# A streaming encoder step on one core: a table of step places for each engine instead of one shared plan

## What is computed

```
for each of 2 layers:
  u = rmsnorm(x) @ w_in                     # one projection, split over three head groups
  oa = softmax(q1 k1) v - lam softmax(q2 k2) v        # group A, 6 heads, block-causal mask
  score = sum_h w_h relu(qi_h . ki);  sel = top_k(score, 256)
  ob = softmax(q k[sel]) v[sel]                       # group B, 5 heads, keys picked by an indexer
  S, oc = gated linear recurrence in blocks           # group C, 5 heads
  x += concat(rmsnorm(oa), ob, rmsnorm(oc) silu(g)) @ w_out
  a, gate = rmsnorm(x) @ w_up;  x += (silu(conv3(a)) * gate) @ w_down
y = rmsnorm(x)
```

## Time and profile before

| | |
|---|---|
| median of 3 runs | 3888.84 us (3884.03 to 3899.14) |
| the profiled execution | 3897.18 us, span 3895.3 us |
| TensorE busy | 3691.7 us, 95% |
| VectorE, ScalarE, GpSimd busy | 2065.7, 1263.7, 761.1 us |
| mean granted clock of TensorE | 0.971 |
| DMA | 339.55 MB |

### The profile page before, as it was taken

How to read it: one execution, slowest core, us unless ns; L and a number is a source line. 1 busy time by engine, 2 the same in 40 slices (tenths; PEclk the granted TensorE clock), 3 DMA queues, 4 the chain that set the end, 5 groups by cost and what they waited for, 6 DMA issues and landing times. The chain is left out here.

```text
span 3895.3 us, 54785 instructions
## 1 busy us (share of the span) xinstructions
PE 3691.7 (95%) x21676; PEld 2940.2 (75%) x21676; DVE 2065.7 (53%) x4711; ACT 1263.7 (32%) x2918; POOL 761.1 (20%) x812
## 2 busy tenths in 40 slices
PE   7997799999999999999999999999999999999998
PEld 5775577678777777778867777787777787788887
DVE  1674564376635554428846555067644654553442
ACT  1124333245243432222244333145344433312221
POOL 2200211111010133202000013323001011453334
PEclk9998898999999999999999999999999999999999
DMA  4332222322121223233231222335112122342223
GB/s 146 97 109 65 77 87 78 103 95 92 56 84 36 78 89 96 80 113 124 72 101 48 82 68 88 107 114 162 55 48 87 30 84 65 96 141 87 67 84 94
DMA packets 151608, 339.55 MB, mean 87 GB/s; under 512 B 30312, under 2 KB 68648, under 8 KB 138040
## 3 DMA queue, kind: packets, MB, share of 16 engines
q1 hardware_dynamic: 151352, 336.04, 27.7%
HBM read 299.31 MB, written 36.68 MB: 86 GB/s over the span
## 5 line engine op out<-in xcount | busy, mean ns | idle before, releaser
L1042 PE MATMUL PS<-xn,wring 128*128 128x272 f32 (+1 forms) x7168 | 1693.7, 396 | 24.9 <-DVE xn L1598 15.1
L1042 PEld LDWEIGHTS PS<-xn,wring 128*128 128x128 f32 x7168 | 1381.1, 195 | 288.6 <-issue 35.3
L2010 POOL TENSOR_TENSOR xT<-xT,res 128x272 f32<-128x272 f32 (+1 forms) x320 | 255.6, 800 | 2251.3 <-ACT res L1325 2211.4
L1042 PE MATMUL PS<-dense,wring 128*128 128x256 f32 (+1 forms) x2816 | 654.6, 390 | 10.4 <-ACT res L1325 5.1
L1042 PEld LDWEIGHTS PS<-dense,wring 128*128 128x128 f32 x2816 | 532.1, 192 | 106.7 <-issue 10.3
L1325 ACT ACTIVATE res<-PS 128x272 f32<-128x272 f32 (+1 forms) x320 | 123.6, 388 | 539.5 <-PE PS L1042 514.0
L1063 PE MATMUL PS<-wring,xn 128*128 128x256 f32 (+1 forms) x1152 | 266.3, 392 | 2.3 <-ACT dense L1339 2.3
L1063 PEld LDWEIGHTS PS<-wring,xn 128*128 128x128 f32 (+1 forms) x1152 | 214.4, 188 | 49.5 <-issue 5.9
L1042 PE MATMUL PS<-catT,wring 128*128 128x272 f32 (+1 forms) x1024 | 235.5, 391 | 4.7 <-issue 2.7
L1333 ACT ACTIVATE dense<-PS 128x256 f32<-128x256 f32 (+1 forms) x176 | 68.3, 389 | 521.7 <-PE PS L1042 480.9
L1042 PEld LDWEIGHTS PS<-catT,wring 128*128 128x128 f32 x1024 | 195.2, 192 | 44.8 <-issue 11.3
(11 more groups left out here) (243 smaller groups left out, 4492.7 us busy)
## 6 DMA issues: line engine op xcount, KB each, us to landing
wring<-in_wu SPq DMA_DIRECT2D x88, 1024.0 KB, 4.9
wring<-in_wf SPq DMA_DIRECT2D x88, 512.0 KB, 3.7
wring<-in_wo SPq DMA_DIRECT2D x64, 512.0 KB, 3.6
wring<-in_wd SPq DMA_DIRECT2D x96, 320.0 KB, 2.9
wring<-in_wd SPq DMA_DIRECT2D x64, 384.0 KB, 3.1
wring<-in_wn SPq DMA_DIRECT2D x16, 1024.0 KB, 5.5
kv<-out_projT SPq DMA_DIRECT2D x48, 256.0 KB, 4.2
out_projT<-dense SPq DMA_DIRECT2D x40, 272.0 KB
```

The source lines that it names most:

```text
L1042: mm = nc.tensor.matmul(PS[:, dbank(t.g0), 0:cw], wtile(t.q, i), rhs, start=(kk == a), stop=(kk == b - 1))
L2010: nc.gpsimd.tensor_tensor(x, x, res[:, i % NRES, 0:cw], ALU.add).then_inc(s_res, 1)
```

## The change

`PLAN` becomes a dictionary of three strings, one for each engine, and `both` takes the engine's name. TensorE's string comes from `TURNS_BEFORE`, which gives for each of the 540 steps the number of dense turns ahead of it. ScalarE's and VectorE's add the entries of `SCALAR_LATER` and `VECTOR_LATER` to it (a negative entry puts the step ahead). The old string remains as `LOADS` and feeds `STEPS_AT` alone, so SyncE's order is what it was; GpSimd's program isn't touched, and no instruction is added or removed.

```diff
-PLAN = "".join((
+LOADS = "".join((
...
-for _x in PLAN:
+for _x in LOADS:
...
+TURNS_BEFORE = {
+    ("X", 0): (
+        30, 31, 31, 31, 31, 31, 32, 32, 35, 35, 35, 35, 35, 35, 35, 38, 38, 41, 41, 41, 42, 49, 51, 51, 52, 52, 52, 52, 52, 52, 53, 54, 54, 54, 54,
+        54, 54, 54, 55, 55, 65, 65, 65, 66, 66, 66, 66, 66, 66,
+    ),
+    ("B", 0): (
+        66, 66, 66, 66, 66, 66, 66, 66, 66, 66, 66, 66, 67, 67, 67, 67, 67, 67, 67, 68, 68, 68, 68, 68, 68, 70, 70, 71, 71, 76, 76, 77, 77, 77, 78,
+        79, 81, 81, 81, 81, 82, 83, 83, 83, 84, 86, 87, 89, 90, 90, 90, 90, 91, 91, 92, 93, 94, 94, 94,
+    ),
...
+SCALAR_LATER = {
...
+    ("C", 0): (
+        -1, 1, 1, 0, -1, 0, -3, 0, -3, -1, -3, 0, 3, -1, 0, -1, -1, -1, -2, -2, -4, -1, 0, -1, 0, -1, -1, -1, -2, -1,
+    ),
...
+def order_of(later):
+    plan, done = "", 0
+    for step in STEPS:
+        for n, d in zip(TURNS_BEFORE[step], later[step] if later else (0,) * len(TURNS_BEFORE[step])):
+            plan, done = plan + "d" * (n + d - done) + "s", n + d
+    return plan + "d" * (len(TURNS) - done)
+
+PLAN = {"pe": order_of(None), "act": order_of(SCALAR_LATER), "dve": order_of(VECTOR_LATER)}
...
-        def both(turns, steps):
-            for x in PLAN:
+        def both(turns, steps, which):
+            for x in PLAN[which]:
...
-                both(dense_tensor(pe), (None for kind, m in STEPS for _ in make[kind](pe, m)))
+                both(dense_tensor(pe), (None for kind, m in STEPS for _ in make[kind](pe, m)), "pe")
```

More of the change, by code:

```diff
@@ new lines @@
+SCALAR_LATER = {
+    ("X", 0): (
+        -4, -1, -1, 7, 7, 8, 9, 9, 6, 6, 6, 6, 6, 6, 6, 3, 3, 1, 1, 1, 1, -6, -6, -6, -6, -6, -6, -6, -1, -1, -1, -1, -1, 0, 3, 3, 3, 3, 2, 4, -6,
+        -6, -5, -6, -4, -2, -2, -2, -2,
+    ),
+    ("B", 0): (
+        -2, -2, -2, -2, -2, -2, -2, -2, -2, -2, 0, 0, -1, -1, -1, -1, -1, -1, -1, -2, -2, -1, 0, 0, 0, -1, 1, 2, 2, -1, -1, 0, 0, 0, -1, -1, -1, -1,
+        -1, -1, -1, 0, 0, 0, 1, -1, 0, -1, -1, 0, 0, 0, 0, 0, 0, 0, 0, 0, 0,
+    ),
+    ("C", 0): (
+        -1, 1, 1, 0, -1, 0, -3, 0, -3, -1, -3, 0, 3, -1, 0, -1, -1, -1, -2, -2, -4, -1, 0, -1, 0, -1, -1, -1, -2, -1,
+    ),
+    ("M", 0): (
+        -1, -1, -2, -4,
+    ),
+    ("X", 1): (
+        -2, -1, 0, 0, 0, 0, 0, 0, 0, 0, 0, -1, 2, 1, -2, 6, 5, 7, 7, 12, 13, 13, 14, 16, 13, 14, 13, 15, 15, 16, 14, 9, 10, 6, 10, 8, 8, 8, 11, 11,
+        13, 11, 13, 17, 21, 15,
+    ),
+    ("B", 1): (
+        11, 8, 6, 0, -1, -1, 0, -1, -1, -1, 0, 0, 0, -1, -1, 0, 1, 0, 4, 0, 0, 0, -1, 0, 0, 0, 0, 0, 0, -1, 1, 0, 1, 0, 1, 0, 1, -1, -1, -1, 1, -1,
+        2, 0, 1, 0, 0, 2,
+    ),
+    ("C", 1): (
+        0, 6, 5, 1, -2, -2, -2, 1, -1, -1, -5, -1, -3, -1, -1, -1, -1, 0, -1, -1, 0, 2, -1, 1, -8, -5, -1, -1, -1, -1,
+    ),
+    ("M", 1): (
+        -1, -1, -2, -2,
+    ),
+    ("X", 2): (
+        -1, -1, -1, -6, -5, -5, -5, -4, -4, -3, 1, 2, 4, 5, 5, 7, 6, 6, 5, 5, 5, 4, 1, -4, -4, -4, -1, 0, 2, 2, 4, 4, 5, 5, 6, 6, 3, 3, 3, 3, 3, 3,
+        6, 13, 12, 11, 7, 4, 4,
+    ),
+    ("B", 2): (
+        4, 3, 1, -1, -1, -1, 1, 0, 0, 0, -2, -2, -2, -2, -2, 0, 0, 0, 0, 0, 0, 0, 0, 0, 0, -1, 0, -1, -1, 0, -1, 0, -1, 1, 1, 0, 0, 0, -1, -2, -1,
+        -1, -1, -1, -1, -1, -2, -2, -1, 0, 0, -1, 0, 0, -1, 1, -1, 0, -1,
+    ),
+    ("C", 2): (
+        2, 1, 1, 0, 0, 0, 0, 0, -2, -3, 0, -1, 0, 0, -1, -1, -1, 5, -1, -1, -1, 3, 3, 0, 1, -1, -3, -3, -3, -4,
+    ),
+    ("M", 2): (
+        -4, 4, 1, 3,
+    ),
+    ("X", 3): (
+        0, 0, -1, -1, 0, 2, 0, -1, -1, -2, -4, -5, -11, -9, -9, -12, -11, -11, -12, -17, -16, -16, -14, -13, -13, -13, -12, -12, -16, -18, -19, -23,
+        -21, -24, -22, -21, -23, -20, -22, -20, -15, -14, -13, -12, -11, -7,
+    ),
+    ("B", 3): (
+        -1, 0, 1, 0, -1, -1, 0, 0, 1, -1, 0, -1, -1, 0, -1, -1, 0, 0, 0, 0, -1, -1, -1, 0, 0, 0, -1, 0, 1, 0, 0, -1, -1, -1, 0, -1, -1, 0, -1, 0, 0,
+        0, 2, 0, 0, 0, 0, 1,
+    ),
+    ("C", 3): (
+        0, 1, 4, 0, -1, -1, 0, -1, -1, -2, -2, 0, -2, 0, -4, -2, -2, -1, -2, 1, 0, -1, -1, -1, -1, -8, -5, -4, -3, -1,
+    ),
+    ("M", 3): (
+        -3, -1, 0, 8,
+    ),
+}
@@ new lines @@
+VECTOR_LATER = {
+    ("X", 0): (
+        -7, -6, -6, -6, -1, 10, 9, 9, 8, 8, 8, 8, 8, 9, 11, 11, 11, 13, 17, 17, 17, 10, 8, 8, 8, 10, 13, 14, 14, 14, 13, 12, 13, 13, 13, 13, 13, 16,
+        15, 15, 5, 5, 5, 4, 4, 4, 4, 4, 4,
+    ),
+    ("B", 0): (
+        4, 4, 4, 4, 5, 5, 5, 5, 5, 5, 5, 5, 4, 4, 4, 4, 4, 4, 4, 3, 3, 3, 3, 3, 3, 1, 1, 0, 1, -3, -3, -3, -3, -3, -4, -2, 1, 1, 2, 2, 7, 6, 10, 10,
+        9, 7, 6, 8, 7, 7, 7, 11, 10, 10, 9, 8, 7, 7, 7,
+    ),
+    ("C", 0): (
+        7, 9, 9, 10, 10, 11, 9, 9, 6, 6, 1, 1, 1, -3, -6, -7, -7, -7, -9, -7, -9, -9, -9, -9, -10, -12, -11, -8, -9, -8,
+    ),
+    ("M", 0): (
+        -8, -8, -10, -9,
+    ),
+    ("X", 1): (
+        -10, -2, -2, -4, -4, -1, 0, 1, 3, 3, 3, -4, -1, 2, 0, 4, 7, 8, 8, 9, 12, 12, 13, 17, 14, 15, 13, 14, 15, 16, 14, 8, 8, 4, 11, 16, 15, 15, 15,
+        15, 15, 15, 15, 15, 19, 11,
+    ),
+    ("B", 1): (
+        7, 4, 4, -2, -3, -3, -1, -2, 0, -1, -2, -1, -1, -1, 5, 5, 11, 9, 8, 4, 2, 1, 2, 1, 0, 3, 1, 0, -2, -2, -2, 10, 13, 11, 7, 2, 2, 1, 0, 1, 0,
+        1, 2, 7, 4, 2, 2, 1,
+    ),
+    ("C", 1): (
+        2, 6, 5, 5, 5, 8, 9, 18, 25, 34, 37, 36, 33, 34, 31, 30, 29, 28, 27, 26, 26, 25, 22, 20, 14, 18, 18, 18, 17, 17,
+    ),
+    ("M", 1): (
+        16, 15, 14, 11,
+    ),
+    ("X", 2): (
+        9, 9, 9, 1, 1, -1, -3, -3, -3, -4, -4, -6, -6, -6, -6, -5, -3, -3, -2, 0, 1, 2, -1, -2, 0, 0, -1, -1, -1, -3, -2, -2, -1, 0, 0, 0, -2, 2, 3,
+        4, 4, 4, 4, 5, 4, 4, 0, -1, 3,
+    ),
+    ("B", 2): (
+        4, 4, 2, 4, 4, 3, 3, 4, 4, 4, 1, 1, 2, 3, 3, 3, 3, 3, 3, 3, 2, 2, 2, 2, 2, 1, 0, 1, 1, 1, 1, 0, -1, 1, -2, 2, 0, -2, 1, 0, 1, 1, 1, 1, 0, 0,
+        0, 0, 0, 0, 0, 1, 0, -1, 1, 0, 6, 6, 5,
+    ),
+    ("C", 2): (
+        5, 3, 3, 0, 0, -2, -2, -2, -4, -3, -1, 6, 4, 2, -3, 0, 1, 1, -4, -3, 2, 3, 5, -4, -4, -4, -4, 0, -4, -7,
+    ),
+    ("M", 2): (
+        -3, 3, 15, 17,
+    ),
+    ("X", 3): (
+        6, 10, 9, 20, 17, 16, 12, 11, 9, 8, 6, 3, -5, -5, -5, -8, -8, -9, -12, -17, -10, -8, -8, -8, -5, -5, -5, -4, -3, -3, -5, -10, -10, -13, -13,
+        -13, -16, -16, -18, -18, -13, -13, -10, -6, -4, -3,
+    ),
+    ("B", 3): (
+        -1, -1, -1, -2, -4, -1, 0, 0, 1, 0, -1, -1, -2, -1, -2, -1, -1, 0, 0, 0, -1, -2, 0, 2, 0, 8, 7, 5, 1, 1, 0, -3, -2, -1, 0, -1, -1, -2, 1, 2,
+        0, -2, 3, 4, 1, -1, -4, -1,
+    ),
+    ("C", 3): (
+        -1, 5, 5, 1, -1, -1, 0, 2, 0, 1, 2, 3, 3, 6, 1, 1, 1, 3, 2, 5, 4, 2, 2, 1, -2, 0, 0, 0, 3, 1,
+    ),
+    ("M", 3): (
+        -1, 2, 2, -5,
+    ),
+}
@@ L2076, in _ @@
                 nc.scalar.activation(lam2, lam2, ACT.Exp).then_inc(s_pre_exp, 1)
-                both(dense_scalar(act), (None for kind, m in STEPS for _ in make[kind](act, m)))
+                both(dense_scalar(act), (None for kind, m in STEPS for _ in make[kind](act, m)), "act")
             @block.vector
@@ L2109, in _ @@
                 dve.wait_ge(s_set, 1)
-                both(dense_vector(dve, step), (None for kind, m in STEPS for _ in make[kind](dve, step, m)))
+                both(dense_vector(dve, step), (None for kind, m in STEPS for _ in make[kind](dve, step, m)), "dve")
 def kernel(**inputs):
```

52 lines of the change are left out of this document (added).

## The result

The changed kernel took 3910.52 us (median of 5 runs, 3907.54 to 3917.24) against 3888.84 us before (median of 5, 3876.45 to 3899.14): ratio 1.0055, 95% interval 1.0040 to 1.0071. It is half a per cent slower where 1.8% faster was forecast, and it lies outside the predicted range. The profiled execution took 3917.24 us with a span of 3915.4.

What follows compares the result with a forecast made beforehand. TensorE, busy 3691.7 of 3895.3 us, was taken to bound the kernel, with time to regain from its standing and lowered clock. Terms summed to 66 us saved, giving 3820 us against the median of 3889; range 3750 to 3890.

Steps and rivals of the forecast that it cites:

- Term 1: Twelve C step 8 groups: ScalarE's copies run earlier, removing 18 of 23.2 us of TensorE waits; bounds 10 and 23.
- rival A: C step 8 waits only move to VectorE and the clock stays down: about 3878 us, 10 saved; chance 0.14.
- Term 2: C windows: TensorE's clock recovers once the step 8 waits go, 25 us saved; bounds 8 and 34.
- Terms 3 and 4: First indexer step, 4 us saved by covering one turn; B0 packed tighter, 6 us saved.
- term 3: First indexer step: one dense turn of TensorE's wait for ScalarE is covered, 4 us saved; bounds 0 and 8.
- rival B: Packed steps B0.0 to B0.25 run at 1.2 GHz, 27 us lost: about 3850 us, 39 saved; chance 0.15.
- Term 5: Norm behind X3.42: half of TensorE's 5.11 us wait for VectorE's scaling goes, 3 us saved; bounds 0 and 5.
- Terms 6 and 7: All other places: 12 us saved with the clock; new waits from moved steps: 2 us lost.
- term 7: New waits from late loads (X3.1) or ScalarE steps ahead of evictions: 2 us lost; bounds 0 and 25.
- Rival C: Held evictions delay stores and loads until the weight ring runs dry: slower, about 3928 us; chance 0.10.
- rival D: Most standing and clock loss goes, terms near their upper bounds: about 3770 us, 120 saved; chance 0.19.
- marks of failure: TensorE's standing falls by less than 25 us, or it falls and mean clock does not rise above 0.975.

Runs made afterwards that it cites:

- e3: Kernel before with only ScalarE's part of each C step 8 one dense turn earlier; 3847.87 us, ratio 0.9898.
- e2: Kernel before with only the attention steps of mixer 2 (B2) at their new places; 3917.14 us, ratio 1.0077.
- e10: Kernel before with ScalarE's C step 8 one turn earlier and C steps 5 to 7 at the new places on every engine; 3900.07 us, ratio 1.0019.
- e6: C and M mixers at the new places, X and B at those of the kernel before; 3872.23 us, ratio 0.9946.
- e7: X and B mixers at the new places, C and M at those of the kernel before; 3934.48 us, ratio 1.0098.
- e5: Changed kernel with B2 at TensorE's new places on all engines, plus two unused products ahead of 24 packed B2 steps; 3904.45 us, ratio 1.0032.
- mixed version: Kernels with old places, ScalarE's C step 8 one turn earlier and new places only in some C and M stretches; ratios 0.9876, 0.9867, 0.9853.
- e12: Old places, ScalarE's C step 8 one turn earlier, new places for M3 and C3 from step 20, unused products in B0; 3835.81 us, ratio 0.9853.

## Why the prediction was wrong

*Term 1, the C step 8: right.* 18 us were forecast, and the waits on lines 1285 and 1290 fell from 23.2 to 2.8 us, 20.4 saved. They did not turn into waits for VectorE's sum, which had been thought even at two turns (rival A); 2.8 us is all that there is of it.

*Term 2, the clock behind those waits: right alone, not in company.* Alone, terms 1 and 2 are e3's 40 us against 43 forecast. In the whole change little of it is left. Over turns 104 to 136, 300 to 380 and 490 to 557 the loss by the clock is 149.9 x 0.03 + 323.4 x 0.04 + 237.2 x 0.03 = 24.5 us. In the profiled execution before it was 172.0 x 0.09 + 327.1 x 0.05 + 233.1 x 0.02 = 36.5, so 12 of 25 are saved; but in e2, with the C steps at their old places, it was 161.0 x 0.02 + 326.4 x 0.05 + 233.6 x 0.03 = 26.5. Most of the 12 is the chance that the table showed for C0, not the change. Other standing, such as that of steps 5 to 7, came where the waits of step 8 had been; that it keeps the clock down is shown only in so far as e10 has both. The C places as a whole gave 21 us (e6) instead of 43.

*Terms 3 and 4, the indexer's first step and B0: about right in sum, the second part of B0 too large.* With X and B alone moved (e7), turns 22 to 104 took 17.5 + 235.7 + 202.0 = 455.2 us; in e2, where they stand as before, 28.3 + 225.0 + 208.6 = 461.9. That is 7 saved against 10 forecast. Turns 22 to 27 fell by 10.8: the 8.3 us of the indexer's first wait and 2.5 of its products, which now stand later. But of the 10.7 more in turns 27 to 70, 4.75 is a wait before turn 28 for the eviction of turn 26, as the term said, and 1.8 are those products. So term 3 gave 8.3 - 4.75 = 3.5 of 4, and the packing cost some 10.7 - 4.75 - 1.8 = 4 instead of 7, although rival B's mark was met: a clock of 0.73 in the first 90 us of B0, which begins at 275 instead of 252. The rest of B0 won 6.6 instead of 13.

*Term 5:* turns 620 to 724 fell by 1.9 us; 3 forecast.

*Terms 6 and 7, other places and new waits: here the prediction failed.* I forecast 12 - 2 = 10 us saved, with 25 as the most that new waits could cost and no price outside B0 for the clock of newly packed steps; they came out at some 68 lost, 27.5 in B2, 12.7 in B1, 5.5 in X1 and the 43 - 21 = 22 by which the C places fell short. With 43, 7 and 2 for the other terms that makes 43 + 7 + 2 - 68 = -16, against 17 lost by e6 and e7 together and 21 in the change itself:

- B2 lost 27.5 us in the profiles and 30 by e2. This is rival B, the packed steps at 1.2 GHz, at a place that I never priced. I worked out how many steps follow another for B0 alone (16 to 22 of the first 26), wrote "hundreds of places" for the rest, and in term 7 said that a packed step hides. In B2 they rise from 13 to 24, with ten at one place where it had been three at most, and the clock goes from 1.00 and 0.99 to 0.86 and 0.92. With e5 the cause is shown.
- The C steps 5 to 7 stood closer. e10 puts that, with VectorE's moved parts, at 47 us beside e3's gain; in the whole change, beside what other moved C steps give, e6 is 19 us short of e3. Nothing in the sum had a term for a step that stands for no other engine, though the row was there: line 1214 stood 9.5 us for "issue" in the waits before.
- B1 took 12.7 us more in e7 (461.3 against 448.6 us, turns 200 to 300; 11.4 more in the change) and X1 5.5 more (turns 136 to 200, 234.1 against 228.6). No experiment takes these apart, but the traces name most of the time as new waits: in turns 200 to 300 of the kernel after TensorE stands 9.7 us where it stood 1.5, the most of it for an eviction (line 1572, 3.3) and for VectorE's softmax (lines 1997 and 1990, 4.1), at a clock of 0.99 or better; in X1 it stands 9.9 where it stood 5.9, 8.8 of it for ScalarE's part of the indexer (line 1593). Which moved step is behind each stays open.

Beside these, X3.1 met its late load as term 7 had it, 5.5 us on line 1277. Rival C, held evictions, is there in its first half: the waits for ScalarE's evictions went from 18.7 to 36.6 us. One of them, in C2, has the picture that the rival drew, an eviction behind a C step that ScalarE had ahead of it and that waited for VectorE:

```profile
2411.96 0.66 ACT L1725 ACTIVATE scr<-scr 64x544 f32<-64x544 f32 x1 [2.23 <-DVE scr L2053]
2412.52 0.63 ACT L1520 ACTIVATE res<-PS 128x256 f32<-128x256 f32 x2
...
2413.03 1.32 PE L1237 MATMUL PS<-dense,wring 128*128 128x256 f32 x5 [2.02 <-ACT res L1520]
```

The 18 us more (3.9 of them the wait before turn 28) are far over the 2 of term 7. Its second half, a weight ring that runs dry, has no part: no wait for a weight tile is in the list. Nor has rival D. Of the marks of failure that the prediction named, the first came: TensorE's standing didn't fall by 25 us but rose by 3.6. The mean clock went down too, 0.971 to 0.965.

The Trainium skill's TensorE: Matmul & The Clock Gate (Part 1) has the throttled clock as the default state, from which activity releases it. I gave the rival that rests on it 0.15, because B0's clock of 0.87 spoke against it. The trace after agrees with the rule: B2 at 0.86 though TensorE stood only 11.1 of 138.3 us there, and at 1.00 once products were added (e5).

## What to carry to other kernels

When one resource's clock follows its own activity, a plan that packs its light steps together pays twice, even where no wait appears: count the steps per place over the whole program, not only where the trace of before has its trouble. Price a rearrangement by its best single piece first (here one number on one engine, 1.0%) and add the rest only stretch by stretch, as the mixed version did (1.2 to 1.5%). Where a light stretch can't be spread, products that nobody uses can be cheaper than the clock that they keep up, as in B2 (e5); in B0, with its 45 us of standing, they didn't make the stretch shorter (e12).

## What was not expected of the hardware

- TensorE's clock fell in a stretch in which it was busy 92% of the time (127.2 of 138.3 us), in many short products with pauses of under 2 us. In the packed part itself:

```profile
1956.00:1981.00 25.00, 18.50 (x116) 10.31 (x114) 11.51 (x50) 10.58 (x35) 1.41 (x2) 0.67 0.23 70
```

The packed part of e5, with the added products:

```profile
1951.00:1973.00 22.00, 17.70 (x150) 12.21 (x150) 10.55 (x46) 10.44 (x34) 0.72 (x1) 1.00 0.28 79
```

- Adding 13 to 17 us of products made a stretch 13 us shorter (283.5 to 270.5) and the kernel 0.4% faster.
- TensorE's pauses of 0.6 to 4.1 us in the C steps that no other engine ends all fall on record 193 or 194 modulo 256 and end 1.2 to 1.6 us after a packet of the instruction queue, in the kernels before, after, e3 and e10 alike. Where 197 products and their loads pass in 2.34 us (3264.22 in e10), a block of 256 is gone in under 2 us, and the pause before the next was 4.14 us.
